# First layer's modulation in four column blocks, each with its part of two projection chunks

## What is computed

```python
cond = jax.nn.silu(c)
mod = (jnp.dot(cond, ada_w[layer]) + ada_b[layer])[:, None, :]
sh1, sc1, g1, sh2, sc2, g2 = jnp.split(mod, 6, axis=-1)
u = x * (1.0 + sc1) + sh1
mix = _mixer(u, w_in[layer], conv_w[layer], gk_w2[layer], gk_b[layer], gla_norm_w[layer], w_out[layer])
x = _layernorm(DEEPNORM_ALPHA * x + (1.0 + g1) * mix, ln1_g[layer], ln1_b[layer])
```

## Time and profile before

| | us |
|---|---|
| median of 3 runs | 2479.08 |
| lowest, highest | 2474.95, 2479.88 |
| the profiled execution | 2479.15 |
| its span | 2477.4 |
| PE busy | 2384.6 (96%) |
| DVE busy | 1738.4 (70%) |
| ACT busy | 1300.5 (52%) |
| POOL busy | 81.0 (3%) |

### The profile page before, as it was taken

How to read it: one execution, slowest core, us unless ns; L and a number is a source line. 1 busy time by engine, 2 the same in 40 slices (tenths; PEclk the granted TensorE clock), 3 DMA queues, 4 the chain that set the end, 5 groups by cost and what they waited for, 6 DMA issues and landing times.

```text
span 2477.4 us, 31241 instructions
## 1 busy us (share of the span) xinstructions
PE 2384.6 (96%) x11448; PEld 1922.4 (78%) x11448; DVE 1738.4 (70%) x1974; ACT 1300.5 (52%) x1661; POOL 81.0 (3%) x135
## 2 busy tenths in 40 slices
PE   7999989999999999999998999999999999999997
PEld 4668866768888888888886888878877887897885
DVE  2588775789999999999986546675467443556556
ACT  2334424458877877777873433554344433444442
POOL 1001000000000000000000000000000000000000
PEclk9999999999999999999999999999999999999998
DMA  9869857659999989989986563355536552337550
GB/s 366 319 233 331 307 210 250 205 175 391 393 325 361 393 310 369 389 310 388 364 299 215 172 211 124 115 195 196 198 134 221 176 209 90 126 112 241 203 187 34
DMA packets 317589, 609.91 MB, mean 246 GB/s; under 512 B 15296, under 2 KB 154592, under 8 KB 310809
## 3 DMA queue, kind: packets, MB, share of 16 engines
q1 hardware_dynamic: 307638, 566.09, 64.5%
q0 software_dynamic: 9552, 41.13, 4.6%
q10 hardware_dynamic: 274, 1.05, 0.1%
HBM read 605.05 MB, written 1.08 MB: 245 GB/s over the span
## 4 chain that ended last, share of the span: by engine, by line
PE 85%; DVE 7%; ACT 3%; DMA 2%; issue 1%; POOL 0%; DVEq 0%; ACTq 0%; SPq 0%
PE G L980 50%; PE A L980 29%; PE TB L980 4%; DMA down<-in_ada_w 1%; PE TB L1468 1%; DVE w_lo L2952 1%; PE TB L1577 1%; DMA down<-in_moe_w_down 1%; PE TB L1002 1%; DVE small L3396 1%; ACT probs L2181 0%; DVE x_tok L3406 0%; DVE l_lo L2913 0%; DVE small L2884 0%; DVE x_tok L3410 0%
## 5 line engine op out<-in xcount | busy, mean ns | idle before, releaser
L980 PE MATMUL G<-w_hi,u_hi 128*128 128x512 f32 x1592 | 621.7, 397 | 4.7 <-ACT u_hi L2523 2.4
L980 PE MATMUL G<-w_hi,u_lo 128*128 128x512 f32 x1592 | 612.1, 391 | 2.9 <-DVE u_lo L3296 2.9
L980 PE MATMUL G<-w_lo,u_hi 128*128 128x512 f32 x1592 | 612.1, 390 | 0.0
L2993 DVE TENSOR_TENSOR w_lo<-wide,w_hi 128x1024 fp32r<-128x1024 f32 x352 | 415.6, 1221 | 13.5 <-ACT w_hi L2249 3.3
L2249 ACT ACTIVATE w_hi<-wide 128x1024 fp32r<-128x1024 f32 x352 | 371.2, 1062 | 89.8 <-PE G L980 43.7
L980 PEld LDWEIGHTS G<-w_hi,u_lo 128*128 128x128 f32 x1592 | 298.7, 188 | 69.3 <-DVE u_lo L3296 5.0
L980 PEld LDWEIGHTS G<-w_hi,u_hi 128*128 128x128 f32 x1592 | 298.6, 188 | 68.9 <-issue 4.1
L980 PEld LDWEIGHTS G<-w_lo,u_hi 128*128 128x128 f32 x1592 | 299.7, 188 | 59.9
L980 PE MATMUL A<-w_hi,hidden_hi 128*128 128x512 f32 x772 | 301.4, 390 | 0.0
L980 PE MATMUL A<-w_hi,hidden_lo 128*128 128x512 f32 x772 | 300.7, 389 | 0.0
L980 PE MATMUL A<-w_lo,hidden_hi 128*128 128x512 f32 x772 | 300.5, 389 | 0.0
(11 more groups left out here) (449 smaller groups left out, 3143.3 us busy)
## 6 DMA issues: line engine op xcount, KB each, us to landing
down<-in_moe_w_down SPq DMA_DIRECT2D x176, 512.0 KB, 8.3
wide<-in_ffn_w_in SPq DMA_DIRECT2D x88, 1024.0 KB, 7.6
wide<-in_moe_w_gate SPq DMA_DIRECT2D x160, 512.0 KB, 8.1
wide<-in_moe_w_up SPq DMA_DIRECT2D x160, 512.0 KB, 9.0
down<-in_ffn_w_out SPq DMA_DIRECT2D x44, 1024.0 KB, 8.5
down<-in_ada_w SPq DMA_DIRECT2D x28, 1024.0 KB, 7.1
wide<-in_w_in SPq DMA_DIRECT2D x24, 1024.0 KB, 7.3
ada_row<-in_ada_w POOLq DMA_DIRECT2D x16, 1024.0 KB, 6.6
```

Source lines behind the costliest of these rows:

```text
L980: return nc.tensor.matmul(o, lhsT, rhs, start=start, stop=stop, skip_group_check=True)
L2993: V.tensor_tensor(w_lo[at % RING][:, :], raw_piece(n, at)[0], w_hi[at % RING][:, :].bitcast(F32), ALU.subtract).then_inc(lo_ready, 1)
```

## The change

Layer 0's start is rewritten. The first 2048 columns of `ada_w` are loaded in four blocks; block i holds, for all 1024 rows, the 256 columns of the shift and the 256 of the scale that belong to features 256i to 256i+255 (2 MB, in runs of 1 KB). Behind each block SP loads the i-th quarter of the first two chunks of `w_in`. PE turns x first; per block it forms the sums (`block_product`), turns them to columns (`block_columns`), and works off the pieces of the two chunks and the low-rank part of the features of the block before (`first_piece`, `low_part`). The bias comes in already turned (`ada_b_cols`, 8 KB instead of 256 KB). The identity is loaded with `c` on ACT's queue. The 16 later rows move to the pieces 8 to 23, one behind each. The table `CHAIN` now places the other work of the mixer, later for layer 0, as before for layer 1. The convolution moves in both layers: its three terms from pieces 18, 20, 20 to 17, 18, 19, its additions from 21, 21 to 20, 21.

```diff
-ADA_AT = (1, 3, 4, 5, 6, 8, 10, 12, 14, 15, 17, 18, 19, 21, 22, 23)
+BLOCKS = 4
+BLOCK_COLS = 512
+ADA_AT = tuple(range(8, 24))
+CHAIN = (dict(decays=9, sums=10, turned=12, scores=13, states=14, last_state=15, out=(17, 18),
+              log=9, exps=(11, 12), turns=14, squares=(19, 20),
+              gates=10, scaled=(11, 12), clear=14, masked=14, joined=15, last_joined=16, mean=(19, 20), normed=(20, 21), rows=(18, 24)),
...
+            def fill_first(n):
...
+                def block(i):
+                    if i == 3:
+                        sp.wait_ge(ada_used, 2)
+                    cols = slice(256 * i, 256 * i + 256)
+                    for s in range(2):
+                        to = slice(256 * s, 256 * s + 256)
+                        if block_at[i] is None:
+                            for h in range(2):
+                                sp.dma_start(down[h][:, :].rearrange("p (k c) -> p k c", k=4)[:, :, to],
+                                             blocks[:, 4 * h:4 * h + 4, s, cols]).then_inc(mini_full[h], 16)
+                        else:
+                            sp.dma_start(block_at[i][:, :, to], blocks[:, :, s, cols]).then_inc(block_full[i - 1], 16)
...
+                for i in range(BLOCKS):
+                    block(i)
+                    if i == 1:
+                        sp.dma_start(con[:, P + 1:], I["con"][:, P + 1:]).then_inc(s_con, 16)
+                    quarter(0, i)
+                    quarter(1, i)
+                released.append((lo_ready, n.lo + 7))
+                released.append((lo_ready, n.lo + 8))
...
-                            fill_mini(arg, 4 + at, 1 + at // KD, at % KD, (7, 8)[at] if at < 2 else 7 + at)
+                            fill_mini(arg, 4 + at, 1 + at // KD, at % KD, max(KD, 7 + at))
...
+                        for k in range(KD):
+                            j = k % 4
+                            last = mm(A[32 * j:32 * j + 32, 0, :], condT[:, k:k + 1].to_broadcast([P, 32]), ada_block(i, k),
+                                      k < 4, k >= 4)
+                        last.then_inc(ada_used, 2)
...
+                    block_product(0)
+                    block_columns(0)
+                    for i in range(1, BLOCKS):
+                        block_product(i)
+                        first_piece(0, i - 1)
+                        block_columns(i)
+                        first_piece(1, i - 1)
+                        low_part(i - 1)
+                    first_piece(0, 3)
+                    low_part(3).then_inc(gla_low, 1)
+                    first_piece(1, 3)
...
+            act.dma_start(con[:, 0:P + 1], I["con"][:, 0:P + 1]).then_inc(s_c, 16)
...
+                    for i in range(BLOCKS):
+                        copy_rows(i)
+                        first_piece(0, i)
+                        rounded(i)
+                        first_piece(1, i)
...
+                    for i in range(BLOCKS):
+                        modulated(i)
+                        first_rest(0, i)
+                        low_rows(i)
+                        first_rest(1, i)
...
-                        if p == 18:
+                        if p == 17:
                             dve.wait_ge(s_gla, 32 * (arg + 1))
                             conv_term(0)
-                            mean_square(0)
+                        if p == 18:
+                            conv_term(1)
                         if p == 19:
-                            mean_square(1)
-                            normed(0)
+                            conv_term(2)
                         if p == 20:
-                            normed(1)
-                            conv_term(1)
-                            conv_term(2)
+                            conv_add(1)
                         if p == 21:
-                            conv_add(1)
                             conv_add(2)
```

More of the change, by code:

```diff
@@ new lines, in _ @@
+                    pe.wait_ge(one_ready, 1)
+                    for k in range(KD):
+                        last = mm(TB[:, 0, k:k + 1], c_row[:, tok(k)], one, True, True)
+                    last.then_inc(c_turned, 1)
+                    pe.wait_ge(s_x, 16)
+                    for t in range(T):
+                        turn_x(0, t, 0)
+                    pe.wait_ge(cond_ready, 1)
+                    block_product(0)
[6 more added lines that the diff above has]
+                        low_part(i - 1)
@@ L2918, in sum_rows, with linear @@
                 dve.wait_ge(ada_used, ADA_ROWS * l + KD * (group + 1))
[L2919 removed]
+                dve.wait_ge(s_bias[group], 64 * l + (64 if group else 16))
                 if group == 1:
[L2921 to L2922 removed]
+                    if l:
+                        dve.wait_ge(ada_turned, BLOCKS + l)
+                else:
                     dve.wait_ge(rows_out, 16 * (2 * l + (1 if group else 0)))
                 V.tensor_tensor(ada_rows[:, :], bank, mod[:, 2 * group, 0:512], ALU.add).then_inc(ada_rows_ready, 1)
[L2926 to L2928 removed]
+            def linear(n, chunks, evac, slots=range(6), between=None, early=2, first=0):
+                for c in range(first, chunks + 1):
                     for q in range(4):
@@ L3657, in read_out @@
                         return V.tensor_copy(dst, gla_bank(c, b))
-                    linear(n, 6, read_out, between=between)
+                    chain = CHAIN[arg]
+                    if arg == 0:
+                        for b in range(2):
+                            dve.wait_ge(g_done, n.g + b + 1)
+                            read_out(0, b).then_inc(g_read, 1)
+                    linear(n, 6, read_out, between=between, first=0 if arg else 2)
                     if arg == 0:
```

277 lines of the change are left out of this document (177 added, 100 removed).

## The result

The changed kernel takes 2483.73 us (median of 14 runs, 2479.48 to 2487.86), the kernel before 2476.82 us over its 14 runs beside them (2474.95 to 2479.88). The ratio is 1.0023, with a 95% interval of 1.0016 to 1.0030, so the change costs some 5.7 us. I had forecast 3.7 us won, at 2475.4 us, with a range that ended at 2483. That stood on a median of 2479.08 us for the kernel before; over 14 runs it is 2.3 us lower, so against its own comparison the forecast missed by 9.4 us (3.7 won forecast, 5.7 lost). The profiled execution took 2484.03 us with a span of 2482.2.

The account below looks back on a forecast made before the run. Loads of 10.4 MB bound the start, PE what follows. Layer 0's last row product 9.0 us earlier, less 4.8 of waits, gives 4.2; less 0.5 in layer 1, 3.7 us faster: 2475.4 us, range 2469 to 2483.

Parts of the forecast that it names:

- The start and p7: Layer 0's start: projection piece p0 at about 23 us; last block landed at 41.2, eighth piece p7 ended at 56.2.
- The price of 1 KB runs: Block loads at layer 0's start: 1 KB runs move 344 GB/s at full share, so blocks take 24.4 us.
- The rival of a clock that falls in every round: Layer 0's block rounds at 1.2 GHz: three give 12 us slower, 2491; chance 0.12, shared with other losses over 5.
- The work behind p7: Layer 0, from the end of p7 to the last modulation row's product: 76.9 us of work remain.
- Wait (1): Layer 0, third later modulation row: lands at 71.7 us, PE wants it at 70.9; 1.3 us, bounds 0 and 3.
- Wait (2): Layer 0, later rows in two slots, row i issued once row i-2 is used: 1.5 us, bounds 0 and 4.
- Wait (3): Layer 0, convolution's shifted-row copies: VectorE waits for them, holding piece p19 by 2.0 us, bounds 0 and 3.5.
- Sum for layer 0: Layer 0: 9.0 us earlier without new waits, less 4.8 us for the three waits, so 4.2 us won.
- Layer 1: Same convolution order there: p19 to p21 held 1.1, 0.9, 0.8 us; net loss 0.5, bounds 2 won, 3 lost.
- waits eat it: Rival: 1 KB runs 2.6 us dearer, three waits at upper bounds; 4 us lost, with layer 1 to 2484; chance 0.14.
- loads that keep up: Rival, layer 0: waits at lower bounds or 1 KB runs free; 6 to 11 us earlier, 2468 to 2473; chance 0.26.

Follow-up runs that it names:

- e3: Changed kernel with the new convolution order one piece later in both layers (terms 17, 19, 20, additions 21, 22); 2480.11 us, ratio 1.0012.
- e4: Kernel before with only the change's convolution order (terms 17, 18, 19, additions 20, 21) in both layers; 2484.73 us, ratio 1.0027.
- e10: Kernel before with the late convolution order (terms 18, 19, 20, additions 21, 22) in both layers; 2479.31 us, ratio 1.0008.
- e1: Changed kernel with the convolution's old order back in both layers (terms 18, 20, 20, additions 21, 21); 2482.03 us, ratio 1.0014.
- e2: Changed kernel with the convolution late in layer 0 alone (terms 17, 20, 20, additions 21, 21), new order in layer 1; 2482.09 us, ratio 1.0019.
- e5: Changed kernel with a third slot for layer 0's later modulation rows, convolution order as in the changed kernel; 2484.33 us, ratio 1.0027.
- e6: Changed kernel with the third row slot and the convolution one piece later (terms 17, 19, 20, additions 21, 22); 2477.37 us, ratio 1.0000.
- e9: e6 with VectorE's gates step of layer 0 one piece earlier (9 instead of 10); 2473.64 us, ratio 0.9984.
- e11: Changed kernel run again unchanged, for a second profile; profiled span 2481.1 us.
- e8: Changed kernel with the third row slot and the six shifted-row copies issued by GpSimd on its own queue; 2485.95 us, ratio 1.0035.

## Why the prediction was wrong, step by step

**The start and p7: right in the numbers, and the 56.2 by luck.** p0 came at 24.21 us (about 23 forecast), the end of p7 at 56.15 (56.2). But I had the block rounds wait for loads, 9 us for 7.6 us of PE, and PE waited for no load from 20.69 to 56.15. A round took 9.2 us of PE (the products of the third and the last block start at 31.55 and 40.72), since a block's product is 16 matmuls and 1.92 us, where I took 1.06. The loads, for their part, came sooner than forecast: 14.38 MB had moved by 41 us, where I had 14.4 MB land by 43.9. So the last block's product started at 40.72, close to the 41.2 that I gave its landing, though no load set that time. The two errors met. The price of 1 KB runs also rests on a wrong reading: the two thirds that I gave them in the stage from 200 to 260 us of the earlier trace rows hold for SP's 10.4 MB, while GpSimd moved 9.8 MB in the same stage, mostly in 8 KB runs. The rate from 20 to 40 us, with runs of 1 and 2 KB mixed, is still near what I took (383 GB/s at a share of 1.07 are 358 for a full one, where the row gave 365). Besides, x landed 8.7 us behind its issue, by the table of issues; one pause of 1.68 us ahead of the second block brought the granted clock down for one round only. The rival of a clock that falls in every round did not come about.

**The work behind p7, 76.9 us: right.** From 56.15 to 145.26 are 89.1 us. Of these 9.1 are waits and 2.4 the slow piece 19, which leaves 77.6, 0.7 over.

**Wait (1), the third row, 1.3 us with bounds 0 and 3:** 2.17 and 1.89 us. Right within its bounds.

**Wait (2), two slots, 1.5 us with bounds 0 and 4:** mis-sized. In the changed kernel it shows 2.90 us (0.85 + 1.32 + 0.73), and what the hold of piece 19 covered comes on top: 5.2 us in e3, over my upper bound. I had compared 8.1 us of DMA with 7.9 us of PE for two steps and concluded that the loads nearly keep up. That holds for the mean, but with two slots the queue can't use its idle time. From 92 to 95 us it moved 3 GB/s:

```profile
92.00:95.00 3.00, 3.00 (x21) 1.66 (x21) 2.54 (x7) 1.06 (x1) 0.00 (x0) 1.00 0.01 3
```

The next row was asked for at 94.31: its slot was in use until 93.06, and ahead of it in SP's queue a half chunk waited for a low half until 93.89. What was not moved there had to go into the stretch with the copies. The kernel before idles there too (74 GB/s from 92 to 94 us), but its rows were spread over 24 pieces, and PE didn't run short.

**Wait (3), the shifted rows, 2.0 us with bounds 0 and 3.5:** this is the step that failed first: the landing times of the copies, 5 and 2 us, which no row showed, and the clock behind the hold, which I put at nothing. The mechanism was as I had put it, and so was its second half, that a held piece also holds the next loads. The size was not. Copies landed, by VectorE's start, 9.8 and 8.0 us behind the last issue in the two profiles (8.2 in e4, 9.1 in e3, 7.8 in e10), where I took 5 for a full queue and 2 for a short one (4.5 and 3.3 in layer 1). I priced a copy by where it stands in the queue. What its landing takes was in no row of before, since VectorE came for it 10 us behind the last issue; that gap was an upper bound and I should have taken it as one. And I left out the clock: a pause of 4 us was followed by a piece of 5.32 us instead of 2.94. The term cost 6.4 us in the first profile (4.0 + 2.4) and 4.8 in the second (3.1 + 1.7).

**Sum for layer 0:** 4.8 us of waits forecast, 11.5 found (9.1 + 2.4), and 0.7 more of work, so the 4.2 us won became 3.15 lost. By the mean of the profiles, 142.3 against 144.2, it is 1.9 lost.

**Layer 1, 0.5 us lost with bounds 2 won and 3 lost:** by the stretch's means, 334.2 and 337.4, it lost 3.2 us. The hold of piece 19 was 2.7 and 1.9 us where I had 1.1, again with a slow piece behind it (4.46 and 4.61 us); the 1.42 us of the earlier trace rows went, as forecast, but the shorter wait behind it stayed (0.66 us). The order acts only from piece 17 on, and from there to `w_out` the changed kernel took 27.33 and 26.69 us against 24.65: 2.7 and 2.0 us are the order's, and the rest of the 3.2 lies where the change does nothing. e1 and e2, with the old and the new order in layer 1, differ by 2.7 us in the whole stretch and by 2.2 from piece 17 on. Where no slow piece followed the hold (e4), the order cost 0.9 us.

Layer 0's 1.9 and layer 1's 3.2 are 5.1 of the 5.7 us that the ratio gives; the rest is within what profiles of one kernel differ by.

**The rivals.** The right one was *waits eat it*, also in what decides it: I named (3), and that a held p19 holds the next loads. It had 0.14, and its price was built from upper bounds that two terms then broke; 5.7 us lost lies just past the 5 at which its class ended. Its sum was also too small: 4 us lost in layer 0 and 3 in layer 1 make 2486, not 2484, and a range up to there would have held the 2483.73. The others, loads that keep up and the clock of the block rounds, did not come about. The clock did play its part, behind single pauses, where I had not looked.

## What to carry to other kernels

A consumer that is moved ahead needs the landing time of what it waits for, and the trace of before has it only as a bound if nobody waited there: take the whole gap between issue and first use as possible. On an engine that works in order, look at what is next in its program behind each wait: here the convolution and the gates were not urgent, the low half behind them was, and with the third slot in place, moving the convolution a piece back was worth some 7 us (e5 to e6) and moving the gates a piece ahead some 4 (e6 to e9). When work is packed more densely, count slots as well as bytes: a ring of two left the queue idle for 3 us and short of time 10 us later. The third slot won nothing while piece 19 was held (e5), some 3 us with the late convolution (e6 against e3), and the kernel got ahead of the one before only with both waits on VectorE out of the way (e9).

## What the runs showed of the hardware

- On-chip copies of 1 MB in all, issued within 6 us beside loads, needed 8 to 10 us more to land, 13 from GpSimd's queue, where the smallest of them was the last. The 16 engines moved 227 to 292 GB/s meanwhile (108 to 116 us of the changed kernel's two profiles). The kernel before still moved 432 and 399 GB/s in these stretches, its copies being issued from 110.62 on behind loads, and 249 from 118 to 120 us.
- Of twelve pauses of PE of at least 2.4 us in layer 0's mixer, over all profiles, eight were followed by slower matmuls (0.63 us instead of 0.39 in the pieces) and a lower granted clock; four were not, one of 3.51 us (e3) among them. Shorter ones could be followed by it too (1.93 us in layer 1 of e11, with a piece of 4.61 us). The same code goes both ways at the start, too. In the changed kernel the first block's product took 1.92 us, with 3.6 for the second; in e3 it was 3.64 for the first and 1.92 for the second, and in e8 and e9 3.64 for both. Where the first took 3.64, the granted clock of the table of stages stood at 1.00 all the same (15 to 19 us), so at the start the matmuls' own times are the better witness. A part of the spread between runs of one kernel may come from this; that it is all of it, I haven't shown.
